# A third buffer for the split rows in the last stage, and the loads of the third and fourth row tile ahead of the last store

## The reference, cut to what matters

```python
pool_out = pool_mixer(u_pool, w_pool[l], pool_scale[l]) * jax.nn.silu(g_pool)
...
attn_out = dsa_attention(q, k, v, qi, ki, wi) * jax.nn.silu(g_attn)
y = jnp.einsum('bse,ed->bsd', jnp.concatenate([pool_out, attn_out], axis=-1), w_out[l])
x = x + gate[:, None, :] * y
```

## Time and profile before

| | us |
|---|---|
| median of 3 runs | 3189.06 |
| lowest and highest | 3187.68, 3195.86 |
| span of the profiled execution | 3189.0 |
| PE busy in it | 2990.2 (94%) |
| DVE busy | 2253.7 (71%) |
| ACT busy | 1624.1 (51%) |
| `phase_out_2`, from its first matmul | 2997.57 to 3189.0 |
| mean granted TensorE clock | 0.979 |

### The profile page before, as it was taken

One profiled execution on the slowest core, in us unless ns is written; L12 is line 12 of the kernel. 1 busy time (PEld: TensorE's weight loads), 2 busy tenths in 40 slices (PEclk: granted clock), 3 DMA queues, 4 the chain that ended last, 5 costly groups with the idle time before them and its releaser, 6 DMA issues. The chain is left out here.

```text
span 3189.0 us, 48176 instructions
## 1 busy us (share of the span) xinstructions
PE 2990.2 (94%) x17460; PEld 2369.3 (74%) x17460; DVE 2253.7 (71%) x3296; ACT 1624.1 (51%) x2947; POOL 231.3 (7%) x519
## 2 busy tenths in 40 slices
PE   6999999999998999999999999999977889998899
PEld 5888788888777866677777777887756666776687
DVE  8888877753677758888878554524378989988543
ACT  5344422232545436777769423211288887887500
POOL 0000000000000001110100000000021321213100
PEclk8999999999999999999999999999989999999899
DMA  4434422244657432111136334232641111011665
GB/s 119 121 109 122 145 67 75 84 141 144 170 171 254 154 131 77 32 37 41 45 92 199 112 96 132 86 132 74 172 98 34 31 28 24 23 36 39 170 183 158
DMA packets 377860, 331.47 MB, mean 104 GB/s; under 512 B 100988, under 2 KB 331900, under 8 KB 371472
## 3 DMA queue, kind: packets, MB, share of 16 engines
q1 hardware_dynamic: 371784, 293.40, 32.4%
q0 software_dynamic: 5120, 34.67, 2.8%
q10 hardware_dynamic: 720, 0.31, 0.1%
HBM read 211.26 MB, written 107.10 MB: 100 GB/s over the span
## 5 line engine op out<-in xcount | busy, mean ns | idle before, releaser
L629 PE MATMUL p_oa_acc<-s_h_a_hi,s_mx_w_hi 128*128 128x512 f32 x768 | 301.8, 393 | 15.2 <-DVE s_h_a_lo L418 9.4
L323 ACT ACTIVATE s_mx_w_hi<-s_mx_raw 128x512 fp32r<-128x512 f32 x224 | 139.1, 629 | 320.6 <-PE p_oa_acc L629 256.8
L629 PE MATMUL p_oa_acc<-s_h_a_lo,s_mx_w_hi 128*128 128x512 f32 x768 | 300.4, 391 | 0.0
L629 PE MATMUL p_oa_acc<-s_h_a_hi,s_mx_w_lo 128*128 128x512 f32 x768 | 300.2, 391 | 0.0
L1598 DVE TENSOR_TENSOR_SCAN s_st_prod<-s_st_soft,s_st_prod 128x512 f32<-128x512 f32 x192 | 234.4, 1267 | 15.9 <-ACT s_st_soft L1525 15.9
L3174 PE MATMUL p_sa_turn<-s_ident,s_sa_arg 128*128 128x128 f32 x1088 | 166.3, 289 | 48.5 <-ACT s_sa_prob L2783 30.9
L1525 ACT ACTIVATE s_st_soft<-p_st_z 128x512 f32<-128x512 f32 (+3 forms) x320 | 153.7, 534 | 112.0 <-PE p_st_z L1650 112.0
L2345 PE MATMUL p_pr_ps<-s_h_hi,s_pr_w_hi 128*128 128x512 f32 (+1 forms) x712 | 195.4, 395 | 1.8 <-PEq L1712 1.2
L2766 ACT ACTIVATE s_sa_arg<-s_sa_arg,s_sa_low_top 128x128 f32<-128x128 f32 (+15 forms) x128 | 155.7, 1218 | 79.6 <-DVE s_sa_low_top L2918 79.6
L460 DVE TENSOR_TENSOR s_mx_w_lo<-s_mx_raw,s_mx_w_hi 128x512 fp32r<-128x512 f32 x224 | 153.5, 685 | 57.8 <-ACT s_mx_w_hi L323 56.3
L2345 PE MATMUL p_pr_ps<-s_h_lo,s_pr_w_hi 128*128 128x512 f32 (+1 forms) x712 | 191.5, 389 | 0.0
(11 more groups left out here) (379 smaller groups left out, 7408.7 us busy)
## 6 DMA issues: line engine op xcount, KB each, us to landing
s_mx_raw<-in_w_in_a SPq DMA_DIRECT2D x128, 256.0 KB, 3.8
s_pb_ada<-in_w_ada SPq DMA_DIRECT2D x16, 768.0 KB, 4.3
s_pr_raw<-in_w_in SPq DMA_DIRECT2D x21, 512.0 KB, 3.9
s_pr_work<-s_pr_stage SPq DMA_DIRECT2D x38, 256.0 KB, 4.2
d_rot_hi<-s_pr_rot POOLq DMA_DIRECT2D x9, 1024.0 KB, 4.3
d_rot_lo<-s_pr_stage POOLq DMA_DIRECT2D x9, 1024.0 KB, 6.2
d_y_t<-s_mx_y SPq DMA_DIRECT2D x16, 512.0 KB, 5.5
s_oa_y_raw<-d_y_t SPq DMA_DIRECT2D x16, 512.0 KB, 4.8
```

The lines of the kernel that those rows point to most:

```text
L323: nc.scalar.activation(w_hi[:, m], raw[g % 2][:, m], ACT.Copy).then_inc(hi_done, 1)
L629: ins = nc.tensor.matmul(bank, w[:, m, k, :], a[:, m, k, :], start=(k == 0 and n == 0), stop=(k == KH - 1 and n == 2))
```

## The change

A third pair of tiles, `third_hi` and `third_lo`, joins the two buffers of `m_hi` and `m_lo`; `hi_of` and `lo_of` hold the three, and tile t uses t % 3 (`SPLIT`). All other buffers stay two deep, `m_raw` and `g_raw` among them. ScalarE's wait becomes one for the product of tile t - 3 (none for tile 2). On VectorE `split(2)` moves ahead of the division of the last attention tile, and behind `finish(t)` stands `split(t + 3)` in place of `split(t + 2)`. On SP the loads of tiles 2 and 3 stand behind the loads of `xin` and ahead of the last attention tile's store and its wait for `divided`; the loop's loads run over t = 2 to 13, each still at the head of its pass.

```diff
-    DEEP = 2
+    DEEP, SPLIT = 2, 3
...
+        third_hi = al.sb("oc_third_hi", [P, KC, P], F32R)
+        third_lo = al.sb("oc_third_lo", [P, KC, P], F32R)
...
+        hi_of, lo_of = (m_hi[:, 0], m_hi[:, 1], third_hi[:]), (m_lo[:, 0], m_lo[:, 1], third_lo[:])
...
+            def load_rows(t):
+                j = t % DEEP
+                sp.wait_ge(m_lo_done, t - DEEP + 1)
+                if tiles[t] in ORDER[LAST - 1:]:
+                    sp.wait_ge(o_out[ORDER.index(tiles[t]) % 2], 16 * (TILES // 2))
+                sp.dma_start(m_raw[:, j], m_v[tiles[t]]).then_inc(m_in[j], 16)
+                sp.dma_start(g_raw[:, j, 0:HALF], gp_v[tiles[t]]).then_inc(m_in[j], 16)
+                sp.dma_start(g_raw[:, j, HALF:], ga_v[tiles[t]]).then_inc(m_in[j], 16)
...
+            for j in range(2):
+                sp.wait_ge(o_out[j], 16 * (TILES // 2 - 1))
+            for t in range(DEEP, 2 * DEEP):
+                load_rows(t)
             sp.wait_ge(divided, TILES)
             sp.dma_start(o_v[ORDER[LAST]], space.o_sb[:, LAST % 2]).then_inc(o_out[LAST % 2], 16)
-            for j in range(2):
-                sp.wait_ge(o_out[j], 16 * (TILES // 2 - 1))
             for t in range(TILES):
                 j = t % DEEP
-                if t + DEEP < TILES:
-                    sp.wait_ge(m_lo_done, t + 1)
...
+                if DEEP <= t < TILES - DEEP:
+                    load_rows(t + DEEP)
                 if t < LAST:
                     sp.wait_ge(added, t + 1)
...
                 act.wait_ge(gated, t + 1)
-                act.wait_ge(product, 2 * (t - DEEP) + 2)
-                nc.scalar.activation(m_hi[:, j], m_raw[:, j], ACT.Copy).then_inc(m_hi_done, 1)
+                if t >= SPLIT:
+                    act.wait_ge(product, 2 * (t - SPLIT) + 2)
+                nc.scalar.activation(hi_of[t % SPLIT], m_raw[:, j], ACT.Copy).then_inc(m_hi_done, 1)
...
-                nc.vector.tensor_tensor(m_lo[:, j], m_raw[:, j], m_hi[:, j].bitcast(F32), ALU.subtract).then_inc(m_lo_done, 1)
+                nc.vector.tensor_tensor(lo_of[t % SPLIT], m_raw[:, j], hi_of[t % SPLIT].bitcast(F32), ALU.subtract).then_inc(m_lo_done, 1)
...
+            split(DEEP)
             dve.wait_ge(spread_in, 32 * TILES)
...
                 finish(t, 0, slice(0, DM))
-                if t + DEEP < TILES:
-                    split(t + DEEP)
+                if t + SPLIT < TILES:
+                    split(t + SPLIT)
```

More of the change, by code:

```diff
@@ L3332, in _ @@
                         cols = slice(half * 512, half * 512 + 512)
-                        for n, (w, a) in enumerate(split_pass_list(w_hi, w_lo, m_hi, m_lo)):
-                            ins = nc.tensor.matmul(acc[t][:, cols], a[:, t, k, :], w[k][:, cols], start=(k == 0 and n == 0), stop=(k == KC - 1 and n == 2))
+                        for n, (w, a) in enumerate(split_pass_list(w_hi, w_lo, hi_of, lo_of)):
+                            ins = nc.tensor.matmul(acc[t][:, cols], a[t][:, k, :], w[k][:, cols], start=(k == 0 and n == 0), stop=(k == KC - 1 and n == 2))
                         if k == KC - 1:
@@ L3343, in _ @@
                     for k in range(KC):
-                        for n, (w, a) in enumerate(split_pass_list(w_hi, w_lo, m_hi, m_lo)):
-                            ins = nc.tensor.matmul(acc[j][:, cols], a[:, j, k, :], w[k][:, cols], start=(k == 0 and n == 0), stop=(k == KC - 1 and n == 2))
+                        for n, (w, a) in enumerate(split_pass_list(w_hi, w_lo, hi_of, lo_of)):
+                            ins = nc.tensor.matmul(acc[j][:, cols], a[t % SPLIT][:, k, :], w[k][:, cols], start=(k == 0 and n == 0), stop=(k == KC - 1 and n == 2))
                     ins.then_inc(product, 1)
```

## The result

The changed kernel takes 3227.65 us (median of 4 runs, 3225.91 to 3232.43), the kernel before 3188.52 us beside it (4 runs). The ratio is 1.0119, 95% interval 1.0104 to 1.0133: 39 us slower. The forecast was 3221.4 us, 3210 to 3232. The profiled execution has a span of 3230.5 us against 3189.0; it is the slowest of the four (3232.43 us).

The account below looks back on a forecast made before the run. TensorE bounds the stage before, 11.12 us a tile; after, VectorE's exposed loads: finish(1) at 3029.1 plus twelve passes of 14.45 gives 3202.5, with tile 15 and tail 3220.2, plus 1.2 for the clock 3221.4 us; range 3210 to 3232.

Parts of the forecast that it names:

- begin to data of tile 2: From the stage's first matmul, 2997.57 us, to the landing of tile 2's early loads, taken as 3018.8 us.
- first break: TensorE's 5.23 us without a matmul ahead of tile 2; forecast to end at 3024.4 us and stay over 4 us.
- TensorE's waits ahead of tiles 6 to 15: TensorE idles some 2.3 us ahead of tile 6, then 3.3 us ahead of each tile, 32 us in all.
- step of the new loop: Time from one finish to the next in twelve passes from finish(1) to finish(13): 14.45 us, against TensorE's 11.12.
- The early loads and the split ahead of the finish: At the stage's start, split(2) and the division precede finish(0); TensorE goes on at 3024.4, nine tenths of a microsecond gained.
- What the later splits lose: From tile 4 on VectorE waits behind finish(t) for a load that begins only then; twelve passes of 14.45 us.
- the ring through VectorE, SP and the DMA: The new loop's closed chain: finish 2.49 us, `added` to data 8.4, split to next finish 3.56; 14.45 us per tile.
- the time from `added` to the data: In each loop pass, from a finish's end to the landing of the last gate part: 8.4 us.
- The half fall added for tile 15: A fallen TensorE clock costs a tile 2.5 us, on the path only in tile 15; half, 1.2 us, added.
- The rival in which TensorE stays cold: Whole tiles run at the lower clock, 21 us each, and TensorE bounds again from tile 6: 3290 us; chance 0.03.
- It does what it is built for: Rival: the first break shrinks to about 0.4 us and the clock stays up, 3181.7 us; chance 0.03.
- Nothing moves: Rival: SP passes its waits sooner, so tile t + 3's load starts early enough; 3188 to 3190 us; chance 0.03.

Follow-up runs that it names:

- e1: The changed kernel with the loop's loads of tile t + 3 issued ahead of the wait for `added` of tile t, one finish earlier; 3191.38 us, ratio 0.9998.
- e2: The changed kernel with all splits back in their old places on VectorE, early loads and third buffer kept; 3193.49 us, ratio 1.0010.
- e3: The changed kernel with only split(2) kept ahead of the division and all later splits in their old places; 3192.53 us, ratio 1.0009.
- e4: The changed kernel with the loads of tile t + 3 behind `added` but ahead of y's store and xin's load; 3197.4 us, ratio 1.0020.
- e5: The changed kernel with one more, unused 512 KB load ahead of the three loads in each of twelve passes; 3247.57 us, ratio 1.0178.
- e8: The changed kernel with the third matmul pass left out in tiles 2 to 15, 32 matmuls a tile for 48; 3229.6 us, ratio 1.0115.
- e7: e6 with the last attention tile's division moved behind split(5) and its store into SP's fifth pass; 3182.39 us, ratio 0.9974.
- e6: e1 with the loads of tiles 2 and 3 issued ahead of the wait for the inverse sums; 3183.72 us, ratio 0.9985.

## Why the prediction was right, point by point

| term | forecast | profile after |
|---|---|---|
| stage begins (first matmul) | 2997.6 | 3000.35 |
| begin to data of tile 2 | 21.2 | 21.25 |
| begin to finish(1) | 31.5 | 31.75 |
| first break | 4.4 | 4.69 |
| TensorE's waits ahead of tiles 6 to 15 | 32 | 26.2 |
| step of the new loop, mean of 12 | 14.45 | 15.03 |
| finish(1) to finish(13) | 173.4 | 180.3 |
| finish(13) to the end | 18.9 | 18.1 |
| span | 3221.4 | 3230.5 |

**The early loads and the split ahead of the finish.** The data of tile 2 came when forecast, but by luck, as the two parts of that number were both off: counted from the stage's begin SP issued the last part after 14.2 us and not 15.0, and it took 7.0 us to land, not 6.2. The break was 0.5 us shorter, not 0.9. Part of the difference is in the split: VectorE waited 1.58 us for `m_hi` where later splits wait 1.2, though ScalarE's instruction took the same 1.06 us; the chain lists the rest as issue.

**What the later splits lose.** This was the deciding step, and it held: twelve waits for the load, the ring through VectorE, SP and the DMA, a step of 14.5 us or more, `scaled` as TensorE's releaser. e1 removes it from one side, e2 and e3 from the other, and e4 and e5 move it by bytes. TensorE's ten waits add up to 26.2 us where 32 were forecast, though the step was longer: six of the ten tiles had a stretch at the lower clock, and a fallen clock comes out of the next gap, as the forecast said (4.72 us ahead of tile 6, 0.87 ahead of tile 7).

**The term that was mis-sized** is the time from `added` to the data, forecast at 8.4 us; its twelve waits average 9.0. Of the twelve steps seven are 14.36 to 14.64 us, mean 14.52, right on the forecast. The other five are 15.27 to 16.05, mean 15.73, and make 6 of the 7 us by which the loop is too long. The queue of SP in a short pass and in the long one behind it (start, us of issuing), each with the landing of its last gate part under it:

```profile
3050.36 0.35 SPq L3278 DMA_DIRECT2D out<-s_oc_y  x1
3050.76 0.43 SPq L3280 DMA_DIRECT2D s_oc_x<-d_xf  x1
...
3053.01 0.51 SPq L3255 DMA_DIRECT2D s_oc_g_raw<-d_p_t  x1
...
s_oc_g_raw<-d_p_t SPq DMA_DIRECT2D x1, 256.0 KB, 5.6
```

```profile
3064.72 0.35 SPq L3278 DMA_DIRECT2D out<-s_oc_y  x1
3065.11 1.12 SPq L3280 DMA_DIRECT2D s_oc_x<-d_xf  x1
...
3067.41 0.65 SPq L3255 DMA_DIRECT2D s_oc_g_raw<-d_p_t  x1
...
s_oc_g_raw<-d_p_t SPq DMA_DIRECT2D x1, 256.0 KB, 7.3
```

What the long pass has and the short one has not is a packet of another queue, just ahead of its burst (the queue's line in the window 3064 to 3065: packets, MB, share of the DMA engines):

```profile
q8 instruction: 1, 0.02, 6.0%
```

Such a 16 KB packet of the instruction queue lies within 1 us ahead of the burst, or in it, in each of the five long passes (3034, 3064, 3109, 3144 and 3184 us), and in none of the seven short ones. In e8, where TensorE has a third fewer instructions, there are three such packets, in passes of 15.57, 14.89 and 16.08 us; the other nine are 14.40 to 14.99. So two of the three are long and one is not. e5's trace says less still for it: it has five such packets too, each ahead of a burst or in it (3036, 3070, 3120, 3160 and 3202 us), and its passes with one average 16.70 us, those without 16.47. Its longest pass, between these two finishes, has none:

```profile
3101.29 1.22 DVE L3320 TENSOR_TENSOR s_oc_y<-p_oc_acc,s_oc_gate 128x1024 f32<-128x1024 f32 x1
...
3118.22 1.22 DVE L3320 TENSOR_TENSOR s_oc_y<-p_oc_acc,s_oc_gate 128x1024 f32<-128x1024 f32 x1
```

What does go with the packet each time is SP's own issuing: where one lies just ahead of the burst, the load of `xin` takes SP 0.69 to 1.48 us, in all eleven cases within the passes of the three traces (after, e5, e8), and 0.43 or 0.44 us otherwise. That alone does not lengthen the pass, as the two queues above show: the last gate part leaves 2.7 us behind the store in both, and it is the landing that differs. The Trainium skill ("DMA: Bandwidth & Descriptors", section "Issuing engines are not separate DMA queues") says that transfers of all issuing engines run on the same 16 DMA engines and interleave; it speaks of SP, ScalarE and GpSimd, and the row above shows an instruction packet taking its share of those 16 engines, 6.0% of them for a microsecond, which is one engine for about that time. That the packet causes the long pass was not tested alone, and e5 does not bear it out: what makes five of the twelve landings longer stays open. Before, such packets were there too and cost nothing: a load was wanted only 11 us after the `added` behind which it was issued, and landed after 8.3.

**The rest of the miss.** 2.8 of the 9.1 us are in the profile ahead of the stage, where the change has nothing; other runs of the changed kernel have spans of 3224.0, 3224.3 and 3227.4. Set against the medians, the forecast of 32.3 us more was 6.8 us short.

**The clock.** The half fall added for tile 15, 1.2 us, was not needed: its 48 matmuls took 11.37 us. The rival in which TensorE stays cold fell: the clock did drop in gaps (0.50 at 3078) or just behind them, and came back each time within the tile. The section of the Trainium skill that the forecast named ("TensorE: Matmul & The Clock Gate", section "Loop structure matters more than you think") has its cold case in a wait for a DMA ahead of every matmul. With 48 matmuls behind each wait the mean here was 0.92, and e8 shows that no time hung on it.

**The rivals on the other side.** "It does what it is built for" needed data by 3014.9 and a landing within 5.1 us of `added`; it got 3021.6 and 8.3 to 10.0. "Nothing moves" needed SP to pass its waits early, and SP issued each store only behind `added`, as at 3050.36. e7 shows that the price of the first was right: with the data early enough it is 0.26% faster (0.17 to 0.36%), 8 to 9 us, where 7.3 had been worked out.

## What to carry to other kernels

When a consumer is moved one step up in a software pipeline, its producer has to move as well: a third buffer for the result gives no lookahead while the input's loads are still issued behind the old event. In a queue that issues in order, ask for each load which event stands ahead of it and which step uses it, and count the steps between; here the count went from one to none, at 3.9 us a tile. And a load of which one waits is priced by all the bytes ahead of it in its burst, so if it can't be asked for earlier it should at least go first (e4: 11.8 us a step for 15.0).

## What the runs showed of the hardware

- While the scatter of 1024 four-byte values, a 256 KB store and the gate row's 512 KB load were in flight, SP needed 7.52 us to issue one 256 KB load that takes 0.51 us in most passes of the loop (e6; 5.42 us in e7). An early load can so cost SP's time rather than save it.
- A 16 KB instruction packet just ahead of a burst goes with 0.69 to 1.48 us for SP to issue one load, for 0.43 (after, e5, e8). With a longer pass it goes in the changed kernel (15.73 against 14.52 us) and hardly in e5 (16.70 against 16.47).
- The clock can fall to its lower level after the gap: gaps of 2.51 and 2.86 us without a matmul were each followed by a stretch at 0.50 that began more than a microsecond into the next tile. The four shorter gaps, up to 1.72 us, had none.
- e4's ten runs scatter over 16 us (3188.94 to 3205.3) and e1's ten over 7, but the 31 runs of the kernel before beside them scatter over 16 as well, so that this is e4's own is not shown. Its loop sits 0.7 us over TensorE's own 11.12, and what it adds in the slower runs was not traced.
